# The last norm of a two-block model: gains as a diagonal in the turns to rows, squares summed by products, last scaling on two engines

## What is computed

```python
def rms_norm(x, g):
    x32 = x.astype(jnp.float32)
    y = x32 * lax.rsqrt(jnp.mean(x32 * x32, axis=-1, keepdims=True) + EPS)
    return (y * g.astype(jnp.float32)).astype(x.dtype)

def swiglu(h, w1, w3, w2):
    return (jax.nn.silu(h @ w1) * (h @ w3)) @ w2

def second_block(x, ...):
    for l in range(DEPTH_2):          # 2 layers
        ...                            # mixer with four branches
        x = x + g_f * swiglu(modulate(rms_norm(x, norm_ffn[l]), sh_f, sc_f),
                             w_ffn1[l], w_ffn3[l], w_ffn2[l])
    return rms_norm(x, final_norm)
```

## Time and profile before

| | before |
|---|---|
| time, median of 3 | 1971.04 us (1968.45 to 1972.79) |
| time of the profiled execution | 1965.51 us |
| its span, first to last instruction | 1963.7 us |
| mean granted TensorE clock | 0.992 of full speed |
| PE busy | 1908.0 us, 97% of the span |
| POOL, DVE, ACT busy | 1103.0, 919.7 and 756.6 us |

### The profile page before, as it was taken

The page is one execution under the profiler, slowest core; times in us unless marked ns, Lnnn a source line. Parts: engine busy times, 40 slices in busy tenths (PEclk is TensorE's granted clock), DMA queues, the critical chain, the costliest instruction groups (busy, mean ns, idle before and its releaser), DMA issues.

```text
span 1963.7 us, 31592 instructions
## 1 busy us (share of the span) xinstructions
PE 1908.0 (97%) x13129; PEld 1639.0 (83%) x13129; DVE 919.7 (47%) x1688; ACT 756.6 (39%) x1212; POOL 1103.0 (56%) x611
## 2 busy tenths in 40 slices
PE   9999999989999999999999999999999999999997
PEld 5588999878887788778878888888788987989997
DVE  7955552363935783742253111114476756262112
ACT  5343453332325522733323222222335536434443
POOL 7345997563535443434443444444468754868885
PEclk8999999989999999999999999999999999999999
DMA  8867766664122132124333323223535331675653
GB/s 195 235 222 235 258 213 234 228 220 159 51 89 65 33 128 65 33 65 140 129 119 118 97 81 123 86 75 112 198 123 148 120 107 44 214 236 174 192 169 100
DMA packets 289491, 276.61 MB, mean 141 GB/s; under 512 B 19802, under 2 KB 276324, under 8 KB 289092
## 3 DMA queue, kind: packets, MB, share of 16 engines
q1 hardware_dynamic: 286804, 271.42, 43.6%
q10 hardware_dynamic: 2192, 2.77, 0.4%
q0 software_dynamic: 352, 0.40, 0.1%
HBM read 266.70 MB, written 4.19 MB: 138 GB/s over the span
## 4 chain that ended last, share of the span: by engine, by line
PE 87%; DVE 7%; ACT 2%; issue 2%; DMA 1%; POOL 1%; SPq 1%; ACTq 0%; DVEq 0%; POOLq 0%
PE gb L2610 19%; PE gb L2611 19%; PE gb L2612 19%; PE gb L1761 3%; PE gb L1759 3%; PE gb L1760 3%; PE gb L1487 3%; PE gb L1489 3%; PE gb L1488 3%; PE mb L1208 1%; PE mb L667 1%; PE gb L667 1%; DMA raw<-in_w_ada 1%; PE mb L1275 1%; DVE mx L1237 1%
## 5 line engine op out<-in xcount | busy, mean ns | idle before, releaser
L2597 POOL TENSOR_TENSOR wl<-raw,wh 128x1024 fp32r<-128x1024 f32 (+3 forms) x448 | 972.8, 2190 | 777.3 <-ACT wh L819 777.2
L819 ACT CAST wh<-raw 128x1024 fp32r<-128x1024 f32 (+3 forms) x452 | 420.1, 939 | 658.2 <-PE gb L2612 381.3
L2610 PE MATMUL gb<-xh,wh 128*128 128x256 f32 (+1 forms) x1856 | 602.1, 324 | 8.4 <-DVE xl L1158 4.6
L2611 PE MATMUL gb<-xl,wh 128*128 128x256 f32 (+1 forms) x1856 | 598.2, 322 | 0.0
L2612 PE MATMUL gb<-xh,wl 128*128 128x256 f32 (+1 forms) x1856 | 598.2, 322 | 0.0
L2610 PEld LDWEIGHTS gb<-xh,wh 128*128 128x128 f32 x1856 | 350.4, 189 | 44.3 <-issue 11.1
L2612 PEld LDWEIGHTS gb<-xh,wl 128*128 128x128 f32 x1856 | 350.4, 189 | 27.6
L2611 PEld LDWEIGHTS gb<-xl,wh 128*128 128x128 f32 x1856 | 350.5, 189 | 27.1
L1759 PE MATMUL gb<-fhh,wh 128*128 128x512 f32 (+1 forms) x352 | 118.4, 336 | 0.0
L1761 PE MATMUL gb<-fhh,wl 128*128 128x512 f32 (+1 forms) x352 | 117.9, 335 | 0.0
L1760 PE MATMUL gb<-fhl,wh 128*128 128x512 f32 (+1 forms) x352 | 117.9, 335 | 0.0
(11 more groups left out here) (478 smaller groups left out, 3009.5 us busy)
## 6 DMA issues: line engine op xcount, KB each, us to landing
raw<-in_w_in SPq DMA_DIRECT2D x62, 1024.0 KB, 5.3
raw<-in_w_ada SPq DMA_DIRECT2D x48, 1024.0 KB, 5.4
raw<-in_w_ffn SPq DMA_DIRECT2D x44, 1024.0 KB, 5.2
raw<-in_mlp_w SPq DMA_DIRECT2D x32, 1024.0 KB, 5.6
raw<-in_w_ffn SPq DMA_DIRECT2D x16, 768.0 KB, 4.6
raw<-in_w_ffn SPq DMA_DIRECT2D x16, 640.0 KB, 4.4
raw<-in_ssm_w_glu SPq DMA_DIRECT2D x8, 1024.0 KB, 6.9
raw<-in_w_out SPq DMA_DIRECT2D x8, 1024.0 KB, 5.1
```

The lines of the kernel that those rows point to most:

```text
L819: nc.scalar.copy(split_half(wh, p, j, h), raw_half(p, it, j, h)).then_inc(hi_ready, 1)
L2597: nc.gpsimd.tensor_tensor(split_half(wl, p, j, h), raw_half(p, it, j, h), split_half(wh, p, j, h).bitcast(F32), ALU.subtract)\
L2610: nc.tensor.matmul(o, H[:, k, :], XH, start=st, stop=False)
L2611: nc.tensor.matmul(o, H[:, k, :], XL, start=False, stop=False)
```

## The change

The turn of a tile to rows multiplies by the gains as well. DVE builds eight matrices `gdiag[:, f, :]` of 128x128, with the gains of tile f on the diagonal, from the identity, and waits for them before tile 0. The turn is then an ordinary float32 product x^T times gdiag, with tile f turned after the first half (15 products) of block f+1, and tile 7 at the end, all in `mb`. `grow` and its DMA are gone.

ACT squares each tile of x in the feature layout as soon as it is complete, into one of two buffers `osq`. PE sums the squares over features by two products with a column of ones for each tile, accumulated over the eight tiles in one column of two PSUM banks: tile f's in the middle of block f+2, ahead of the turn of tile f+1, the last two at the end. A buffer of `osq` is used again once PE has summed it. DVE takes the root from those two columns with the common 12-step `rsqrt` in SBUF. Then ACT scales the rows of tokens 0 to 127 and issues their two stores, and DVE scales those of 128 to 255, with SP's two stores. Neither multiplies by gains.

```diff
@@ final_store
-        FINAL = [(a, h) for a in range(2) for h in range(2)]
-        def final_store(eng, n):
-            a, h = FINAL[n]
-            eng.wait_ge(s_on2, n + 1)
+        def final_store(eng, a, h):
+            eng.wait_ge((s_on1, s_on2)[a], h + 1)
             hs = slice(512 * h, 512 * h + 512)
             eng.dma_start(out[0, a * P:(a + 1) * P, hs], onat[:, a, hs]).then_inc(s_out, 16)
...
-            for n in range(1, len(FINAL), 2):
-                final_store(sp, n)
+            for h in range(2):
+                final_store(sp, 1, h)
             sp.wait_ge(s_out, 16 * 4)
@@ PE
-                ffn2_pe(pe, q["f2", half], T, FL[l][half], final_transposes if half and l == LAYERS - 1 else None)
-
-        def final_transposes(it, j):
-
-            p = L2[LAYERS - 1]["f2", 1]
-            i = 4 * it + j
-            for k in ([i - 1] if i else []) + ([KD - 1] if i == KD - 1 else []):
-                wait_drained(nc.tensor, p, k // 4, k % 4, 1)
-                for a in range(2):
-                    dst = gb[:, 1, a * P:a * P + P] if k == KD - 1 else mb[:, 2 * a + k // 4, (k % 4) * P:(k % 4) * P + P]
-                    ins = nc.tensor.transpose(dst, x[:, k, a * P:a * P + P], ident)
-                if k in (3, 6, 7):
-                    ins.then_inc(s_ot, 1)
+                ffn2_pe(pe, q["f2", half], T, FL[l][half], final_middle if half and l == LAYERS - 1 else None)
+
+                if half and l == LAYERS - 1:
+                    final_sums(pe, KD - 2)
+                    final_transposes(pe, KD - 1)
+                    final_sums(pe, KD - 1)
+
+        def final_transposes(pe, f):
+
+            wait_drained(pe, L2[LAYERS - 1]["f2", 1], f // 4, f % 4, 1)
+            for a in range(2):
+                ins = nc.tensor.matmul(mb[:, 2 * a + f // 4, (f % 4) * P:(f % 4) * P + P], x[:, f, a * P:a * P + P],
+                                       gdiag[:, f, :], start=True, stop=True)
+            if f == KD - 1:
+                ins.then_inc(s_ot, 1)
+
+        def final_sums(pe, f):
+
+            pe.wait_ge(s_oc, f + 1)
+            for a in range(2):
+                ins = nc.tensor.matmul(gb[:, 1 + 2 * a, 0:1], osq[:, f % 2, a * P:a * P + P], ones[:, 0:1],
+                                       start=(f == 0), stop=(f == KD - 1))
+            ins.then_inc(s_fsum, 1)
+
+        def final_middle(i):
+
+            if i >= 2:
+                final_sums(nc.tensor, i - 2)
+            if i >= 1:
+                final_transposes(nc.tensor, i - 1)
@@ ffn2_pe
-                    if after is not None:
-                        after(it, j)
+                        if after is not None and k == kt // 2 - 1:
+                            after(p.body * it + j)
@@ ACT
-                    act.wait_ge(s_fl, FL[l][half])
-                    act.dma_start(grow[:, :], A["final_norm_2"].partition_broadcast(P)).then_inc(s_gain, 16)
                     gemm_act(act, q["f2", half], final_squares)
...
         def final_squares(it, j):
 
-            if 4 * it + j == 5:
-                square_final_part(0)
...
+            if 4 * it + j:
+                square_final_tile(4 * it + j - 1)
+
+        def square_final_tile(f):
+
+            wait_drained(nc.scalar, L2[LAYERS - 1]["f2", 1], f // 4, f % 4, 1)
+            if f >= 2:
+                nc.scalar.wait_ge(s_fsum, f - 1)
+            nc.scalar.activation(osq[:, f % 2, :], x[:, f, 0:SEQ], ACT.Square).then_inc(s_oc, 1)
...
-            square_final_part(1)
-            square_final_part(2)
-            for n, (a, part) in enumerate(FINAL):
-                if n % 2 == 0:
-                    final_store(act, n)
+            square_final_tile(KD - 1)
+            act.wait_ge(s_ot, 1)
+            act.wait_ge(s_rf, 1)
+            for h in range(2):
+                nc.scalar.activation(onat[:, 0, 512 * h:512 * h + 512], mb[:, h, :], ACT.Copy, scale=rs[:, 1, 0:1])\
+                    .then_inc(s_on1, 1)
+                final_store(act, 0, h)
@@ DVE
+                if half and l == LAYERS - 1:
+                    dve.wait_ge(s_fl, FL[l][half])
+                    for f in range(KD):
+                        D1.add(v.tensor_scalar(gdiag[:, f, :], ident, vecs[:, V_FIN2 + f:V_FIN2 + f + 1], None, ALU.mult))
+                    D1.wait()
                 scaled_residual(q["f2", half], 40, 1, lambda p, j, i: unit_view(p, j, T),
...
-            dve.wait_ge(s_oc, 6)
...
+            dve.wait_ge(s_fsum, KD)
+            total = gb[:, 1:4:2, 0:1].rearrange("p a b -> p (a b)")
+            rsqrt(D1, rs[:, 0, 0:2], rs[:, 1, 0:2], rs[:, 2, 0:2], rs[:, 3, 0:2], total, 1.0 / D, EPS)
+            dve.sem_inc(s_rf, 1)
+            dve.wait_ge(s_ot, 1)
+            for h in range(2):
+                v.tensor_scalar(onat[:, 1, 512 * h:512 * h + 512], mb[:, 2 + h, :], rs[:, 1, 1:2], None, ALU.mult)\
+                    .then_inc(s_on2, 1)
```

More of the change, by code:

```diff
@@ L137, in build @@
         gsq = sb("gsq", [P, KD, 2])
-        fsum = rs[:, 3, 8:14].rearrange("p (a c) -> p a c", a=2)
         x, x_at, _ = at("x", [P, KD, SEQ + CTX])
@@ L256, in build @@
         onat = at("onat", [P, 2, D], F32, offset=arena1)[0]
-        grow = at("grow", [P, D], F32, offset=arena1 + 8192)[0]
-        osq = at("osq", [P, 512], F32, offset=arena1 + 12288)[0]
+        gdiag = at("gdiag", [P, KD, P], F32, offset=arena1 + 8192)[0]
+        osq = at("osq", [P, 2, SEQ], F32, offset=arena1 + 12288)[0]
         sqr2 = over_pr("sqr2", [P, 4, 512])
@@ L385, in build @@
         s_ot = sem("output_transposed")
-        s_oc = sem("output_copied")
+        s_oc = sem("output_tile_squared")
         s_out = sem("output_stored")
-        s_on2 = sem("output_part_ready")
-        s_gain = sem("final_gain_loaded")
+        s_on2 = sem("second_output_part_ready")
+        s_on1 = sem("first_output_part_ready")
         s_x1 = sem("residual_added")
@@ L447, in build @@
         s_res = sem("residual_complete")
+        s_fsum = sem("final_squares_summed")
+        s_rf = sem("final_root_ready")
         s_squ = sem("square_summed")
@@ L1861, in layer_act @@
             act.wait_ge(s_res, 4 + l)
-        def final_view(a, part):
-            return (mb[:, 2 * a, :], mb[:, 2 * a + 1, 0:3 * P], gb[:, 1, a * P:a * P + P])[part]
         def final_squares(it, j):
-            if 4 * it + j == 5:
-                square_final_part(0)
[L1872 to L1880, removed]
+            if 4 * it + j:
[5 more added lines that the diff above has]
+            nc.scalar.activation(osq[:, f % 2, :], x[:, f, 0:SEQ], ACT.Square).then_inc(s_oc, 1)
         def ffn_pair0(l, half, i):
@@ L3196, in _ @@
                 layer_dve(dve, D1, l)
-            dve.wait_ge(s_oc, 6)
-            total = rs[:, 3, 0:2]
-            step(v.tensor_reduce(total, fsum[:, :, :], AX_X, ALU.add))
-            step(v.tensor_scalar(rs[:, 0, 0:2], total, 1.0 / D, EPS, ALU.mult, ALU.add))
-            rsqrt_beside(D1, rs[:, 0, 0:2], rs[:, 1, 0:2], gb[:, 3, 448:450], gb[:, 3, 456:458], last=rs[:, 2, 0:2])
-            dve.wait_ge(s_gain, 16)
-            for a, h in FINAL:
-                for part in range(h, 2 * h + 1):
-                    src = final_view(a, part)
-                    c = (0, 512, 512 + 3 * P)[part]
-                    cs = slice(c, c + src.shape[1])
-                    ins = v.scalar_tensor_tensor(onat[:, a, cs], src, rs[:, 2, a:a + 1], grow[:, cs], ALU.mult, ALU.mult)
-                    if part == 1:
-                        D1.add(ins)
-                if h:
-                    D1.wait()
-                ins.then_inc(s_on2, 1)
+            dve.wait_ge(s_fsum, KD)
[6 more added lines that the diff above has]
+                    .then_inc(s_on2, 1)
 _INS = ["x", "p", "norm_mix", "norm_ffn", "norm_ple", "norm_final", "ssm_lam_re", "ssm_lam_im", "ssm_log_dt",
```

## The result

The changed kernel took 1980.44 us in the median of six executions (1975.89 to 1986.08), the kernel before 1970.20 beside it (1966.72 to 1972.79). The ratio is 1.0044 with a 95% interval from 1.0027 to 1.0062. Beside the experiments it was run six times more: 1979.53 us, ratio 1.0052 (1.0037 to 1.0067). It is slower, by half a percent, and both intervals lie above 1. The forecast was 1978.2, in a range from 1972.5 to 1981.5.

A forecast was written before the change was run, and what follows sets the result against it. TensorE (PE), busy 97% of the span, was taken to bound the kernel until its last product, then a serial tail. Products +4.6, wait +5.2 and tail -2.6 gave +7.2, median 1978.2 us, range 1972.5 to 1981.5.

The forecast's parts named there:

- Products: PE ahead of block 7's last product: seven diagonal turns and six pairs of sums replace six transpose pairs, +4.6 us.
- Rival D: Products on PE cheaper than in the other norms: 1975.1 with the stall, 1969.9 without; chance 0.08.
- Diagonals: DVE ahead of tile 0: four gdiag instructions each wait for a POOL instruction, four run free; tile 0's residual at 1932.6.
- Rival C: DVE's diagonals ahead of tile 0 not held by POOL: only +2.0, 1973.0 us; chance 0.14.
- The wait on PE: PE in the middle of block 1 waits for tile 0's drain before its turn, until 1933.1: +5.2 us.
- The clock: PE after its stall in block 1: the forecast took full clock; half pace would lose up to 1.6 us more.
- rival B: PE stalls in block 1, then runs at half clock, losing up to 1.6: +8.8, 1979.8 us; chance 0.27.
- The tail: From tile 7's residual to the end: 8.7 us where it was 11.3, so -2.6 us.
- from the last issue to the end 2.4: Last part of the tail: 1963.7 - 1961.27 = 2.4 us, taken over from the kernel before.
- the likeliest case: Whole kernel, forecast as summed, with PE's stall and no fall of the clock: +7.2, 1978.2 us; chance 0.48.
- D with the stall: Cheaper products on PE, with PE still waiting for tile 0: +4.1, 1975.1 us; three quarters of a chance of 0.08.
- The chances: Whole kernel: slower 0.77, within about 0.2% (3.9 us) 0.20, faster 0.03; three quarters of D counted as within.

The follow-up runs named there:

- the early diagonals: Changed kernel with the eight diagonals built one at a time behind the first eight fhl of the last layer, not ahead of tile 0: 1975.64 us, ratio 1.0018.
- the version that reads PSUM: Changed kernel with the eight diagonals built at the same place from a copy of the identity in PSUM: 1972.03 us, ratio 1.0010.
- half the bytes: Kernel with the early diagonals, each of four stores carrying only 256 of its 512 columns: 1974.82 us in one execution, tail 8.19.
- additions with two inputs in SBUF: From a version without the added products and diagonals, ACT multiplying by gains and squaring, DVE adding squares, against the changed kernel: 1968.58 us, ratio 0.9994.
- the diagonals alone: Kernel before plus the eight diagonals, which nobody reads, between the last fhl and tile 0: 1976.58 us, ratio 1.0026.
- the version with plain transposes: Changed kernel with transposes by the identity for the gdiag products, without the diagonals, last norm's gains left out: 1970.70 us, ratio 1.0002.

## Where the prediction was right and where not

- **Products.** Predicted +4.6, measured +4.58 with the early diagonals. The predicted period of 4.45 between residuals is that of the trace with the early diagonals; in the changed kernel it is 4.41 to 4.44 behind the slow stretch. Within it a pair of sums costs less than the 0.45 counted (0.36) and the product behind the turn 0.08 more than others, which wasn't counted; they cancel, and that is luck. Rival D (cheaper products) is out.
- **Diagonals.** Predicted: four held, about 1.6 each, four free, tile 0's residual 8.3 after the start of the last `fhl`. Measured 1.60, 1.60, 1.57, 1.57 and four at 0.27, and 7.65. The mechanism and the count held. Of the 0.65 too much, 0.45 is in the held ones (POOL's four end 1931.93 - 1925.18 = 6.75 after the mark, counted were 7.2) and 0.2 in the free ones (0.9 from there to the residual, counted 1.1). Rival C (not held) fell, and the version that reads PSUM shows where it would have been right.
- **The wait on PE.** Predicted 5.2, measured 4.65: the same 0.6, since PE came to its turn as reckoned.
- **The clock.** This is the step that failed. The forecast went without a fall of the clock and gave it to rival B, with 1.6 us. The trace has it: 6.93 for wait and clock together, less 4.65, is 2.28. The 17 products from 1934.60 on account for 17 x 0.094 = 1.6 of it, the turn and the products next to them at half pace for the rest. The reason given against B was that the earlier trace rows show 4.5 us of idleness at full clock before it fell, and that the wait is at the edge. In this wait it fell 2.9 after PE's last product (1928.87 to 1931.8), as it did in the changed kernel's tail (1966.46 to 1969.3). One row of a stretch was taken for the least that is needed, and it was not. B's own price of 1.6 was short as well: it was taken from a stretch of 3.2 at half clock, and here it was 6.8, in 5.2 of which PE worked.
- **The tail.** Predicted 8.7, measured 9.3, so -2.0 for -2.6. Everything up to the last issue came out (+1.72 for 1.8, +4.19 for 4.15, +6.05 for 6.1 to 6.4). The term that failed is "from the last issue to the end 2.4": it is 3.25, because the four stores now leave in such quick succession that their bytes queue; with half the bytes it is 2.1.
- **Sum.** 4.58 + 6.93 - 2.0 = 9.5 for the forecast 7.2. Two terms were short by together 2.9 (2.28 for the clock, 0.6 for the tail), and there was 0.6 too much for the wait. By its own list it was rival B, 1979.8, that came. The direction held with the likeliest case as with B, and the range held because it reached beyond B. That the likeliest case came within 2.2 of the median 1980.44 is partly luck: it was added to a median before of 1971.04, and the kernel before, run beside the changed one, took 1970.20; against that one the change costs 10.2 where 7.2 was forecast.
- **The chances.** A slip that changed nothing: D with the stall is +4.1, above the 3.9 that counts as slower, so by the prediction's own terms three quarters of D belong to "slower" and a quarter to "within", 0.81 for 0.77.

## What to carry over

An instruction put on an idle engine is not free because the engine is idle: ask which engine at work at that moment can hold it, how many instructions of that engine stand in a row, and who waits behind it. Where a wait of several us on TensorE may come, count the half clock behind it too: here 2.3 us more were lost with a wait of 4.65, and 5.91 - 4.11 = 1.8 more with one of 4.11. And when a tail is made shorter, recompute what its last transfers wait for: the four stores here, issued closer together, were bound by their bytes.

## What the runs showed of the hardware

- A tensor_scalar on DVE with its input in SBUF, 128x128, takes 0.27 alone and 1.57 to 1.60 beside 128x640 instructions of POOL in a row (2.43 and 2.44 beside 128x1024): each waits for one POOL instruction. The same instruction with its input in PSUM takes 0.27 a piece (2.16 for eight) beside the same POOL work. So the memory of the input matters, and an output in SBUF alone is not enough to be held. Input in SBUF with output in PSUM is not shown.
- The Trainium skill (GPSIMD Engine Reference, Key points) says that DVE contends with GpSimd in a two-port mode or with two inputs in SBUF. The additions with two inputs in SBUF were held (four of six took 1.58 to 1.84 where the last one, without POOL, took 0.42), which agrees. The diagonals have one tensor input and were held too (1.57 to 1.60), so by that rule they ran in the two-port mode; no run here shows the mode itself.
- The granted clock fell 2.9 us after TensorE's last work in two places of the changed kernel, and 4.6 after it in the tail of the kernel before (1953.4 to 1958.0). With the diagonals alone it fell at 1942.1, 4.3 us after the wait began and 0.2 after PE had gone on. In the tail of the version with plain transposes it fell after 1.3 (1960.0 to 1961.3). In the stage it was at half for 3.4 us with the diagonals alone and for 6.8 in the changed kernel, during 1.6 of which PE was still waiting. What decides between 1.3 and 4.6 stays open. The Trainium skill (TensorE: Matmul & The Clock Gate, What's actually happening) calls the chip's watch on activity free-running, so that the moment of a change varies with where the work falls in it. That agrees with the spread, and none of these runs tests it.
- The four last stores move 1.05 MB at some 410 GB/s in the changed kernel.
